# Second layer's attention in a two-layer kernel: scores one step sooner, last projection tile in pieces, second head's weighting on GpSimd

## What is computed

```python
q_d, k_d, v_d = ...                      # DSA: 8 heads of 64, one shared key and value
idx_score = einsum(relu(q_i @ k_i), w_i) # indexer scores, causal
sel = top_k(idx_score, 64)               # keys that a query may see
o_dsa = masked_softmax(q_d @ k_d[sel] * s) @ v_d[sel]

proj = h @ w_in                          # q_nsa is the last 512 columns read here: tiles pj5, pj6
q_n = rope(rms_norm(q_nsa))              # NSA: 8 query heads, 2 key heads
o_cmp = masked_softmax(q_n @ k_c * s) @ v_c      # compressed keys, 15 of them
o_slc = masked_softmax(q_n @ k_slc * s) @ v_slc  # 4 blocks of 64 tokens: with 256 tokens all are selected
o_win = masked_softmax(q_n @ k_win * s) @ v_win  # window of 512: all causal keys
o_nsa = o_cmp * g[0] + o_slc * g[1] + o_win * g[2]
out = concat(o_dsa, o_nsa) @ w_out       # tiles ao0, ao1
```

## Time and profile before

| | |
|---|---|
| median of 3 runs | 1182.74 us |
| lowest, highest run | 1181.01, 1182.83 us |
| span of the profiled execution | 1178.0 us (its own time is not given apart; the runs lie 3.0 to 4.8 us above this span) |
| busy: PE, PEld | 1127.1 us (96%), 841.9 us (71%) |
| busy: DVE, ACT, POOL | 549.5 us (47%), 309.0 us (26%), 25.4 us (2%) |
| mean granted TensorE clock | 0.993 |
| DMA | 241.92 MB, mean 205 GB/s |

### The profile page before, as it was taken

One profiled execution on the slowest core, in us unless ns is written; L12 is line 12 of the kernel. 1 busy time (PEld: TensorE's weight loads), 2 busy tenths in 40 slices (PEclk: granted clock), 3 DMA queues, 4 the chain that ended last, 5 costly groups with the idle time before them and its releaser, 6 DMA issues.

```text
span 1178.0 us, 16972 instructions
## 1 busy us (share of the span) xinstructions
PE 1127.1 (96%) x6932; PEld 841.9 (71%) x6932; DVE 549.5 (47%) x1171; ACT 309.0 (26%) x722; POOL 25.4 (2%) x43
## 2 busy tenths in 40 slices
PE   7999999999999999999999999889878989999998
PEld 6689888988777888875555554376756858997443
DVE  2344344414535585442222222236886535678555
ACT  4360010135313301142111110134475242221000
POOL 0000000000000021000000000010000000000000
PEclk9999999999999999999999999999989999999999
DMA  9951211322388544557999999932410413454440
GB/s 378 403 223 72 72 72 72 139 78 106 112 325 334 210 162 188 211 226 283 425 426 424 426 425 426 367 108 85 145 36 2 179 64 115 150 208 180 178 143 36
DMA packets 34731, 241.92 MB, mean 205 GB/s; under 512 B 3946, under 2 KB 4202, under 8 KB 6364
## 3 DMA queue, kind: packets, MB, share of 16 engines
q1 hardware_dynamic: 33500, 234.46, 50.2%
q0 software_dynamic: 720, 3.12, 0.7%
q10 hardware_dynamic: 432, 3.23, 0.7%
HBM read 239.74 MB, written 1.05 MB: 204 GB/s over the span
## 4 chain that ended last, share of the span: by engine, by line
PE 88%; ACT 4%; DVE 4%; DMA 2%; SPq 1%; issue 1%; DVEq 0%; ACTq 0%
PE bank L1406 20%; PE bank L1403 11%; PE bank L1789 10%; PE bank L1383 8%; PE bank L2147 8%; PE bank L1816 5%; PE bank L1454 4%; PE bank L1751 3%; PE bank L1758 2%; DMA arena<-in_stream 2%; PE bank L1374 2%; PE bank L1474 1%; PE bank L1639 1%; PE bank L1642 1%; PE bank L1587 1%; PE bank L2124 1%
## 5 line engine op out<-in xcount | busy, mean ns | idle before, releaser
L1406 PE MATMUL bank<-ring,arena 128*128 128x256 f32 x784 | 174.2, 379 | 1.0 <-ACT arena L1226 0.7
L1406 PEld LDWEIGHTS bank<-ring,arena 128*128 128x128 f32 x784 | 148.1, 190 | 21.3 <-ACT arena L1226 1.0
L818 ACT ACTIVATE arena<-bank 128x256 f32<-128x256 f32 x90 | 32.4, 381 | 194.1 <-PE bank L1406 159.8
L1383 PE MATMUL bank<-ring,arena 128*128 128x256 f32 x320 | 71.0, 380 | 0.3 <-DMA ring<-in_stream 0.3
L1383 PEld LDWEIGHTS bank<-ring,arena 128*128 128x128 f32 x320 | 60.3, 190 | 9.6 <-issue 0.8
L1403 PE MATMUL bank<-arena,ring 128*128 128x128 f32 x528 | 63.0, 275 | 0.0
L1403 PEld LDWEIGHTS bank<-arena,ring 128*128 128x128 f32 x528 | 61.7, 192 | 0.5
L1789 PE MATMUL bank<-ring,arena 128*64 128x256 f32 x512 | 57.0, 381 | 0.0
L1383 PE MATMUL bank<-ring,hTl 128*128 128x256 f32 x256 | 56.6, 379 | 0.0
L1383 PEld LDWEIGHTS bank<-ring,hTl 128*128 128x128 f32 x256 | 48.3, 190 | 8.1 <-issue 1.9
L1789 PEld LDWEIGHTS bank<-ring,arena 128*64 128x64 f32 x512 | 36.0, 137 | 24.1 <-issue 6.7
(11 more groups left out here) (517 smaller groups left out, 1877.3 us busy)
## 6 DMA issues: line engine op xcount, KB each, us to landing
ring<-in_stream SPq DMA_DIRECT2D x163, 1024.0 KB, 6.9
arena<-in_stream SPq DMA_DIRECT2D x38, 1024.0 KB, 12.9
hTl<-in_stream SPq DMA_DIRECT2D x9, 1024.0 KB, 11.4
hTc<-in_stream SPq DMA_DIRECT2D x9, 1024.0 KB, 13.3
consts<-in_consts ACTq DMA_DIRECT2D x1, 3081.0 KB, 16.4
arena<-in_mem SPq DMA_DIRECT2D x2, 512.0 KB, 5.4
arena<-in_x SPq DMA_DIRECT2D x1, 1024.0 KB, 19.2
arena<-in_ctx SPq DMA_DIRECT2D x1, 1024.0 KB, 24.1
```

The costliest lines, as they stand in the source:

```text
L818: ins = act.activation((p[:, 0, :], p[:, 1, :], first)[n], b, ACT.Copy)
L1383: mm = pe.matmul(b[:, 256 * i:256 * i + 256], h[:, k, 128 * i:128 * i + 128], w[:, k, :], start=(k == 0), stop=(k == KD - 1))
L1406: mm = pe.matmul(b, lhs(*source, k), rhs[:, k, :], start=(start and k == 0), stop=(k == 3), skip_group_check=True)
```

## The change

TensorE computes `pj6` in two halves (`token_chunk`, L1454), each behind a step's scores, and its loop becomes: scores of `s`, transposes of `s - 3`, values of `s - 4`. ScalarE, VectorE and TensorE get a new order at the start. The four products of a step are shared: VectorE makes the two of the first head, GpSimd the two of the second, after VectorE's reciprocal; ScalarE's exponentials wait for GpSimd's products of two steps before. The compressed scores go to banks 6 and 7, one step later, and the top-k's last round comes sooner. Two semaphores of the router in the first layer are merged. The core of the diff:

```diff
+            pool.wait_ge(gates_ready, 1)
+            for m in range(STEPS):
+                pool.wait_ge(pair_recip, m + 1)
+                for i, (a, z) in enumerate(TILES):
+                    r = pair_sum[:, m % 2, 2 + i:3 + i]
+                    pr = sS[m % 3][:, 1, a:z]
+                    if m < H2:
+                        h = 2 * (m // 2) + 1
+                        ins = pool.tensor_scalar(pr, pr, r, gates[:, i, h, 1 + m % 2:2 + m % 2], ALU.mult, ALU.mult)
+                    else:
+                        ins = pool.tensor_scalar(pr, pr, r, None, ALU.mult)
+                ins.then_inc(second_norm, 1)
...
             def pair_exps(s):
                 act.wait_ge(s_max, s + 1)
+                if s >= 2:
+                    act.wait_ge(second_norm, s - 1)
...
             pair_exps(1)
+            pair_exps(2)
+            pair_turned(0)
             project(6)
             query_squares(1)
-            pair_turned(0)
-            turned_heads(3)
-            pair_exps(2)
+            pair_turned(1)
+            pair_exps(3)
             heads_root(7, (8, 16))
             preload(ACT.Exp)
-            pair_turned(1)
-            for s in range(3, STEPS + 2):
+            turned_heads(3)
+            for s in range(4, STEPS + 2):
...
             def pair_turn(m):
-                pe.wait_ge(pair_norm, m + 1)
                 for half in range(2):
+                    pe.wait_ge((pair_norm, second_norm)[half], m + 1)
...
-            token_rows("pj6", tile(), h1T)
             pe.wait_ge(s_max, 1)
             pair_scores(2)
-            pe.wait_ge(sum_taken, NO["pj6"] + 1)
+            w = tile()
+            b = fresh("pj6")
+            token_chunk(b, w, h1T, 0)
+            token_chunk(b, w, h1T, 1)
+            pe.wait_ge(sum_taken, NO["kcT"] + 1)
             pair_turn(0)
             pe.wait_ge(s_max, 2)
             pair_scores(3)
+            token_chunk(b, w, h1T, 2)
+            token_chunk(b, w, h1T, 3).then_inc(sum_ready, 1)
+            pair_turn(1)
             pe.wait_ge(heads_ready, 5)
-            pe.wait_ge(pt_taken, 2)
             turn_heads(3)
+            pe.wait_ge(sum_taken, NO["pj6"] + 1)
+            pair_values(0)
             pe.wait_ge(sum_taken, NO["hT3"] + 1)
-            pair_turn(1)
-            pair_values(0)
-            for s in range(4, STEPS + 3):
+            for s in range(4, STEPS + 4):
                 if s < STEPS:
                     pe.wait_ge(s_max, s - 1)
+                    if s == 5:
+                        compressed_scores()
                     pair_scores(s)
-                if s in (8, 9):
-                    compressed_turn(s - 8)
-                if s - 2 < STEPS:
-                    pair_turn(s - 2)
-                pair_values(s - 3)
-                if s == 9:
+                if s == 4:
+                    continue
+                if s in (9, 10):
+                    compressed_turn(s - 9)
+                if s - 3 < STEPS:
+                    pair_turn(s - 3)
+                pair_values(s - 4)
+                if s == 10:
...
             def pair_weighted(m):
                 dve.wait_ge(probs, m + 1)
-                W(dve.reciprocal(pair_sum[:, m % 2, :], pair_sum[:, m % 2, :]))
-                for half in range(2):
-                    for i, (a, z) in enumerate(TILES):
+                dve.reciprocal(pair_sum[:, m % 2, :], pair_sum[:, m % 2, :]).then_inc(pair_recip, 1)
+                dve.wait_ge(pair_recip, m + 1)
+                for i, (a, z) in enumerate(TILES):
...
             pair_masked(0)
             pair_masked(1)
+            top_round()
             pair_weighted(0)
+            pair_masked(2)
             pair_weighted(1)
-            top_round()
+            best_masked()
+            pair_masked(3)
+            pair_weighted(2)
+            queries_means(1)
             queries_turned(1)
-            for s in range(2, STEPS + 1):
-                if s == 4:
-                    queries_root(1)
+            queries_root(1)
+            pair_weighted(3)
+            for s in range(4, STEPS + 1):
                 if s < STEPS:
                     pair_masked(s)
                 if s == 4:
+                    continue
+                if s == 5:
                     compressed_masked()
-                elif s == 5:
+                pair_weighted(s - 1)
+                if s == 6:
                     compressed_weighted()
```

More of the change, by code:

```diff
@@ L1026, in _ @@
             act.activation(ge, ge, ACT.Exp).then_inc(rt_exp, 1)
-            act.wait_ge(rt_dv, 1)
-            act.activation(r2[6], r2[5], ACT.Exp).then_inc(rt_ev, 1)
+            act.wait_ge(rt_sub, 2)
+            act.activation(r2[6], r2[5], ACT.Exp).then_inc(rt_exp, 1)
             taken.one()
@@ L2015, in _, with compressed_scores @@
             pair_scores(3)
+            token_chunk(b, w, h1T, 2)
+            token_chunk(b, w, h1T, 3).then_inc(sum_ready, 1)
+            pair_turn(1)
             pe.wait_ge(heads_ready, 5)
-            pe.wait_ge(pt_taken, 2)
             turn_heads(3)
+            pe.wait_ge(sum_taken, NO["pj6"] + 1)
+            pair_values(0)
             pe.wait_ge(sum_taken, NO["hT3"] + 1)
-            pair_turn(1)
-            pair_values(0)
-            for s in range(4, STEPS + 3):
+            def compressed_scores():
+                for j in range(NT):
+                    for hh in range(4):
+                        for par in range(2):
+                            r = slice(64 * par, 64 * par + 64)
+                            h = 2 * hh + par
+                            at = 384 + 64 * j + 16 * hh
+                            mm = pe.matmul(bank[6 + par][:, at:at + NCMP], RT(4 + h // 2)[r, 128 * j:128 * j + 128],
+                                           kcT[r, h // 4, 0:NCMP], start=True, stop=True)
+                            if (j, hh) == (1, 3):
+                                mm.then_inc(cs_ready, 1)
@@ L2023, in _ @@
+            for s in range(4, STEPS + 4):
                 if s < STEPS:
                     pe.wait_ge(s_max, s - 1)
-                    if s == 6:
+                    if s == 5:
+                        compressed_scores()
+                    if s == 7:
                         pe.wait_ge(cs_sub, 1)
-                    if s == 4:
-                        for j in range(NT):
-                            for hh in range(4):
-                                for par in range(2):
-                                    r = slice(64 * par, 64 * par + 64)
-                                    h = 2 * hh + par
-                                    at = 384 + 64 * j + 16 * hh
-                                    mm = pe.matmul(bank[4 + par][:, at:at + NCMP], RT(4 + h // 2)[r, 128 * j:128 * j + 128],
-                                                   kcT[r, h // 4, 0:NCMP], start=True, stop=True)
-                                    if (j, hh) == (1, 3):
-                                        mm.then_inc(cs_ready, 1)
@@ L2875, in _, with best_masked @@
             rounds = Count()
+            def best_masked():
+                W(dve.tensor_scalar(ibias, iacc, -2e38, -BIG, ALU.is_gt, ALU.mult))
+                W(dve.tensor_tensor(ibias, ibias, C("causal"), ALU.add))
             def top_round():
@@ L2885, in top_round @@
                 settle()
-                if rounds.n == 8:
-                    W(dve.tensor_scalar(ibias, iacc, -2e38, -BIG, ALU.is_gt, ALU.mult))
-                    W(dve.tensor_tensor(ibias, ibias, C("causal"), ALU.add))
             for h in range(H2):
@@ L2973, in _ @@
             queries_turned(0)
+            queries_means(0)
             top_round()
@@ L2994, in pair_weighted @@
                 dve.wait_ge(probs, m + 1)
-                W(dve.reciprocal(pair_sum[:, m % 2, :], pair_sum[:, m % 2, :]))
-                for half in range(2):
-                    for i, (a, z) in enumerate(TILES):
-                        r = pair_sum[:, m % 2, 2 * half + i:2 * half + i + 1]
-                        pr = sS[m % 3][:, half, a:z]
-                        if m < H2:
-                            h = 2 * (m // 2) + half
-                            ins = dve.tensor_scalar(pr, pr, r, gates[:, i, h, 1 + m % 2:2 + m % 2], ALU.mult, ALU.mult)
-                        else:
-                            ins = dve.tensor_scalar(pr, pr, r, None, ALU.mult)
+                dve.reciprocal(pair_sum[:, m % 2, :], pair_sum[:, m % 2, :]).then_inc(pair_recip, 1)
+                dve.wait_ge(pair_recip, m + 1)
+                for i, (a, z) in enumerate(TILES):
+                    r = pair_sum[:, m % 2, i:i + 1]
+                    pr = sS[m % 3][:, 0, a:z]
+                    if m < H2:
+                        h = 2 * (m // 2)
+                        ins = dve.tensor_scalar(pr, pr, r, gates[:, i, h, 1 + m % 2:2 + m % 2], ALU.mult, ALU.mult)
+                    else:
+                        ins = dve.tensor_scalar(pr, pr, r, None, ALU.mult)
                 ins.then_inc(pair_norm, 1)
```

22 lines of the change are left out of this document (9 added, 13 removed).

## The result

The change takes 1185.08 us (median of 20 runs, 1180.17 to 1188.76), the kernel before 1181.9 us beside it (20 runs, 1179.35 to 1184.84). The ratio is 1.002, 95% interval 1.0011 to 1.003: slower by some 0.2% (2.4 us by the ratio, 3.2 by the medians), and surely not faster. The runs of the change scatter along one line, the mean granted clock of the run: the five with 0.983 or less took 1186.6 to 1188.8 us, the three with 0.989 or more 1180.2 to 1182.0.

A forecast was written before the change was run, and what follows sets the result against it. It took waits between engines, none alone filling a step, to bound the second layer's attention. Order -0.8, clock +2.0 and GpSimd beside VectorE +1.07 gave +2.3 us on 1182.74: 1185.0 us, range 1180.0 to 1188.0.

The forecast's parts named there:

- The stage's four parts: Scores 2 to scores 4, TensorE's run from there, VectorE's work to exponentials 7, and the rest to the output projection.
- TensorE's chain: Scores 4, compressed scores, scores 5 and transposes 2 in a row: 4.6 us, plus 2.0 for a lower clock.
- VectorE's chain: Masking 5 to masking 7, with weightings and compressed pieces between, ahead of exponentials 7: 9.65 us, plus 1.07 for GpSimd.
- The late copy: ScalarE copies hT3 after the root's two table loads; scores 4 start at 866.1, not 863.35, after idles of 3.7 and 2.1.
- The clock: Idle TensorE lowers its clock for the chain from scores 4: between 0 and 4.6 us, taken as 2.0.
- GpSimd beside VectorE: VectorE waits one GpSimd instruction, 0.53 us, in each of two weightings ahead of exponentials 7: 1.07 us.
- From step 7 on: Exponentials 7 to output projection: 24.24 us less the 3.19 wait at exponentials 10, plus 1.0 for late transposes, 22.05.
- The order without its prices: The new order up to the output projection, without clock and GpSimd costs: -0.8 us.
- GpSimd as a new wait: Rival: TensorE waits for GpSimd's slower two-factor products, 1186.4 to 1187.8 us; chance 0.20, shared with a clock staying down.
- The late tile without prices: Rival: no clock or GpSimd cost, only the -0.8 us is left, 1181.9 us; chance 0.17.
- The full pipeline: Rival: from exponentials 4 ScalarE alone sets the pace, -5.5 us, 1177.2 us; chance 0.13.

The follow-up runs named there:

- the kernel with products around `hT3`: The change plus 13 and 7 useless matmuls in TensorE's two idle stretches around hT3's wait: 1180.99 us, ratio 0.9983 to the kernel before.
- without GpSimd: The change with all four weighting products of a step back on VectorE, none on GpSimd: 1185.48 us, ratio 1.0019 to the kernel before.
- the kernel with products in three places: The change plus useless matmuls, 7 ahead of the second head turn's wait, 13 and 7 around hT3's: 1179.02 us, ratio 0.9975 to the kernel before.
- the whole tile with products: The change with hT3's copy and rotation first, pj6 whole, useless matmuls in three waits, a second factor in GpSimd's one-factor products: 1178.30 us, ratio 0.9965 to before.
- the first two experiments: The kernel before with GpSimd making the second head's products: 1182.96 us; the change with VectorE making all four: 1185.48 us.
- before with products: The kernel before plus useless matmuls, 7 ahead of the second head turn, 7 and 4 ahead of turns 2 and 3: 1179.61 us, ratio 0.9973.
- GpSimd's share alone: The kernel before, old order, with GpSimd making the second head's products and the router's semaphores merged: 1182.96 us, ratio 1.0002.

## Why the prediction was right, and where its terms were not

1185.0 was forecast and 1185.08 measured. The mechanism came as described, but that the numbers agree to 0.1 us is luck. The stage's four parts were off by -0.7 (up to scores 4: 17.35 for 18.04), +1.2 (TensorE's chain: 7.83 for 4.6 + 2.0), -1.2 (VectorE's chain: 9.66 for 9.65 + 0.1 + 1.07) and +1.5 (the end: 23.51 for 22.05), +0.8 together. And the base, 1182.74 from three runs, lay 0.8 above the 1181.9 that before took beside the change.

- **The late copy: right.** 18.04 us from scores 2 to scores 4 were worked out, 17.35 came; idle 3.7 and 2.1 were forecast, 3.85 and 0.51 came. The second was 1.6 shorter: 0.9 because `hT3` and step 0's values between them ran at half clock and ended later, 0.7 because the copy came sooner than worked out.
- **The clock: right in kind, mis-sized.** I took half of the chain at half clock, 2.0. All of it was: 7.83 us against 4.6 planned, 3.2 more, so the term was 1.2 too small. The upper bound of 4.6 was too high because the full-clock chain itself is shorter than the sum of its rows: 4.2 us in the kernel with products around `hT3` (867.75 to 871.92), 3.6 less than 7.83. That the idle time is what brings the clock down here is shown by the products, which fill it and change no other work.
- **VectorE's chain to exponentials 7: right.** 9.65 us were worked out; from the chain's end at 877.40 to 887.06 are 9.66, with whatever GpSimd costs in it. VectorE runs through all of it without a wait, and without GpSimd the same stretch took 10.71.
- **GpSimd beside VectorE: wrong, 1.07 us too much.** The two products take 0.06 us longer beside GpSimd, about 0.1 for two weightings. The row I went by has two tensor inputs; these one-input products lost 0.06 us where 0.53 was assumed. The Trainium skill ("SBUF — State Buffer", section "SBUF: two separate sides") makes the blocking depend on the mode or the second input; here the trace shows no blocking of a whole instruction's length (GpSimd's take 0.546 and 0.583).
- **From step 7 on: the order right, a fall of the clock left out.** 22.05 forecast, 23.51 measured. The wait at exponentials 10 went as said. But the clock fell a second time, behind the idle 1.81: turns 11 and the last values took 1.54 and 2.23, against 0.88 and 1.57 in the kernel with products in three places, 1.3 in all. That kernel has the same idle of 1.81 there, with no products in it, and its clock stayed up:

```profile
896.33 0.90 PE L1987 MATMUL bank<-consts,arena 128*128 128x128 f32 x6 [1.81 <-ACT arena L1230]
...
897.97 0.88 PE L1987 MATMUL bank<-consts,arena 128*128 128x128 f32 x6
898.77 1.57 PE L2001 MATMUL bank<-arena 128*64 128x256 f32 x16
```

All nine profiles with the changed loop have that idle (1.81 or 1.82); the clock fell behind it in two, the change's and that of the whole tile with products. So the 1.3 belongs to this execution more than to the order.
- **The order without its prices, -0.8: right by the best measure there is.** At full clock the stage is 0.95 us shorter than before's, and the ratios are level within some 2 us.
- **The rivals.** GpSimd as a new wait fell with the first two experiments: a pair takes 1.1 us, or 1.65 with one factor, and no engine waits over 0.2 us for it. The late tile without prices describes the change with products (1179.0, and level with before with products), not the change. The full pipeline did not come; masking 7 still holds up exponentials 7.

What stays open: the profiled stage of before has a clock of 0.94 and that of the change 0.85, each in one execution, and the falls move from run to run (before's profiled span has a clock of 0.993, as high as any of its runs listed; the change's 0.983 is near its lowest). The 2.1 us that the ratios with products give are the better number, but their intervals leave some 2 us either way. So the fall of the clock in the change is shown; that it is the whole of the 0.2% is likely, not shown. That they change nothing but the clock is shown for the rows of the stage, not for every wait.

## What to carry to other kernels

Where one engine is busy 96% of the span, read the idle stretches ahead of its dense chains, not only their sum: behind an idle stretch of 3.85 us the lower clock cost another 3.6 here, nearly as much again. A result that starts the next chain (here a copy of 0.58 us) goes ahead of work that is needed later (a root with two table loads of 1.28 us each). And useless matmuls in a wait that can't be removed are worth trying, in both versions that are compared, or the clock is mistaken for the order.

## What had not been expected of the hardware

- GpSimd's product with **one** factor is slower than with two: 0.747 and 0.919 us (128x128, 128x256) against 0.546 and 0.583. With a second factor of 1.0 the same products took 0.467 and 0.506. It was off the path here.
- Products that nobody reads lowered the time of every order they were put in, by the ratios: before by some 3 us, the change by 4 (two places) and 5 (three), the whole tile by 2 (there with the second factor, and with intervals that overlap).
- The clock's falls are not a matter of the order alone: the same wait of 2.03 us ahead of the second head turn left the clock at 1.00 in the profile of before and took it to 0.50 in that of GpSimd's share alone, whose order is the same.
